# State-space stage of a two-block kernel: the next head's decay sums moved into the unit between two heads, the masked sums behind it, the output last

## What is computed

```python
xbc = silu(causal_depthwise_conv_2(xbc, conv_w, conv_b))
xs, b_in, c_in = jnp.split(xbc, [...], axis=-1)
a_cs = jnp.cumsum(a_dt, axis=-1)                      # one row per head
decay = jnp.exp(jnp.where(causal, a_cs[..., :, None] - a_cs[..., None, :], -jnp.inf))
cb = jnp.einsum('bclgn,bcsgn->bcgls', c_c, b_c)
y_diag = jnp.einsum('bcgjls,bcsgjp->bclgjp', cb[:, :, :, None] * decay, xdt)
decay_from_start = jnp.exp(a_cs).transpose(0, 1, 4, 2, 3)
y_off = jnp.einsum('bclgn,bcgjpn->bclgjp', c_c, prev) * decay_from_start[..., None]
y = (y_diag + y_off) + xs * d_skip
g = y * silu(z)
g = g * rsqrt(mean(g * g, axis=-1) + EPS) * norm_g    # per group of 256 channels
out = g @ w_out
```

## Time and profile before

| | |
|---|---|
| timed runs, median (lowest, highest) | 2892.21 us (2890.09, 2893.98) |
| the profiled execution, its own time | 2889.11 us |
| its span, first to last instruction | 2887.3 us |
| granted TensorE clock, mean | 0.944 of full |
| PE busy | 2724.0 us (94%) |
| DVE, ACT, POOL busy | 1184.7, 979.8, 925.4 us |
| state-space groups | about 1150 to 1612 us of the span |
| PE idle ahead of line 609 | 27.8 us, 15 times |

### The profile page before, as it was taken

The page is one execution under the profiler, slowest core; times in us unless marked ns, Lnnn a source line. Parts: engine busy times, 40 slices in busy tenths (PEclk is TensorE's granted clock), DMA queues, the critical chain, the costliest instruction groups (busy, mean ns, idle before and its releaser), DMA issues.

```text
span 2887.3 us, 35961 instructions
## 1 busy us (share of the span) xinstructions
PE 2724.0 (94%) x15144; PEld 2314.9 (80%) x15144; DVE 1184.7 (41%) x1641; ACT 979.8 (34%) x1482; POOL 925.4 (32%) x381
## 2 busy tenths in 40 slices
PE   4999999889999987989999999999979999999999
PEld 3777778667777767989988999999957677778887
DVE  5444442254444326676666431122343444422111
ACT  3333333333333333334434332233333433433222
POOL 2334344143343432222222334444320000244443
PEclk9999999999999998999999999999975766999999
DMA  3333233133332321111211223333210000133332
GB/s 114 90 92 104 85 111 88 51 100 96 96 100 91 97 78 51 53 52 59 59 52 52 76 82 93 92 92 89 77 51 8 15 8 15 54 93 95 95 95 88
DMA packets 61280, 215.65 MB, mean 75 GB/s; under 512 B 8128, under 2 KB 8512, under 8 KB 61120
## 3 DMA queue, kind: packets, MB, share of 16 engines
q1 hardware_dynamic: 55440, 199.78, 23.5%
q10 hardware_dynamic: 5680, 13.58, 1.4%
HBM read 211.24 MB, written 2.10 MB: 74 GB/s over the span
## 4 chain that ended last, share of the span: by engine, by line
PE 89%; DVE 6%; ACT 2%; issue 1%; ACTq 0%; POOL 0%; DMA 0%; DVEq 0%
PE psum L344 73%; PE psum L939 1%; PE psum L905 1%; PE psum L877 1%; PE psum L436 1%; PE psum L446 1%; PE psum L881 1%; PE psum L629 1%; PE psum L903 1%; PE psum L941 1%; PE psum L356 1%; PE psum L632 1%; PE psum L922 1%; PE psum L584 1%; DVE sb_scale L1483 1%
## 5 line engine op out<-in xcount | busy, mean ns | idle before, releaser
L324 POOL TENSOR_TENSOR sb_w_lo<-sb_w_raw,sb_w_hi 128x1024 fp32r<-128x1024 f32 x377 | 925.2, 2457 | 1939.9 <-ACT sb_w_hi L1055 1939.6
L344 PE MATMUL psum<-sb_h_hi,sb_w_hi 128*128 128x512 f32 (+1 forms) x2648 | 828.9, 355 | 74.6 <-DVE sb_h_lo L1492 45.9
L344 PE MATMUL psum<-sb_h_lo,sb_w_hi 128*128 128x512 f32 (+1 forms) x2648 | 801.1, 344 | 0.0
L344 PE MATMUL psum<-sb_h_hi,sb_w_lo 128*128 128x512 f32 (+1 forms) x2648 | 798.1, 343 | 0.0
L1055 ACT ACTIVATE sb_w_hi<-sb_w_raw 128x1024 fp32r<-128x1024 f32 x377 | 395.3, 1054 | 608.0 <-PE psum L344 458.7
L344 PEld LDWEIGHTS psum<-sb_h_hi,sb_w_hi 128*128 128x128 f32 x2648 | 466.5, 193 | 145.9 <-issue 60.6
L344 PEld LDWEIGHTS psum<-sb_h_lo,sb_w_hi 128*128 128x128 f32 x2648 | 464.3, 193 | 63.4 <-issue 7.5
L344 PEld LDWEIGHTS psum<-sb_h_hi,sb_w_lo 128*128 128x128 f32 x2648 | 463.8, 193 | 57.2
L344 PE MATMUL psum<-sb_mix_hi,sb_w_hi 128*128 128x264 f32 (+1 forms) x1424 | 416.9, 338 | 11.5 <-DVE sb_mix_lo L2193 5.8
L344 PE MATMUL psum<-sb_mix_lo,sb_w_hi 128*128 128x264 f32 (+1 forms) x1424 | 414.9, 337 | 0.0
L344 PE MATMUL psum<-sb_mix_hi,sb_w_lo 128*128 128x264 f32 (+1 forms) x1424 | 414.0, 337 | 0.0
(11 more groups left out here) (268 smaller groups left out, 2680.6 us busy)
## 6 DMA issues: line engine op xcount, KB each, us to landing
sb_w_raw<-in_weights SPq DMA_DIRECT2D x377, 512.0 KB, 3.6
sb_decay<-in_decay ACTq DMA_DIRECT2D x16, 640.0 KB, 3.9
sb_resid<-in_x ACTq DMA_DIRECT2D x1, 2048.0 KB, 11.7
out<-sb_resid SPq DMA_DIRECT2D x8, 256.0 KB, 2.0
sb_table<-in_rope_table ACTq DMA_DIRECT2D x1, 264.0 KB, 3.5
sb_s<-in_positions ACTq DMA_DIRECT2D x1, 256.0 KB, 5.7
sb_cols<-in_cols ACTq DMA_DIRECT2D x1, 158.5 KB, 7.1
sb_resid<-in_meta ACTq DMA_DIRECT2D x1, 64.0 KB, 11.8
```

Source lines behind the costliest of these rows:

```text
L324: e.tensor_tensor(g.w_lo[:, u % 4, :], g.w_raw[:, u % 2, :], g.w_hi[:, u % 4, :].bitcast(F32), ALU.subtract).then_inc(S["w_lo"], 1)
L344: mm = e.matmul(g.psum[0:m, at + b, 0:wd], w[:, slot, P * i:P * i + m], xs[:, tile, c:c + wd], start=first and n == 0, stop=last and n == 2)
```

## The change

In `pe_ssd` alone, in the loop over heads. The unit of eight blocks (48 matmuls) is cut into two halves of four blocks. The sums of decays of the next head stand between the halves; they stood behind the whole unit. The masked sums of the next head stand right behind the unit (at head 0 behind the total); they stood behind the output. The output of the head stands last. In the last group the pieces of the output projection are cut likewise. Nothing else moves, on no engine.

```diff
         for h in range(HG):
             if not last:
-                pe_ssd_unit(g, e, grp + 1, h)
+                pe_ssd_unit(g, e, grp + 1, h, range(4))
             elif h < 2:
-                pe_ssd_out(g, e, h, 0).then_inc(S["unit"], 1)
+                pe_ssd_out(g, e, h, 0, range(4))
             else:
-                pe_ssd_out(g, e, h - 2, 1, range(6))
+                pe_ssd_out(g, e, h - 2, 1, range(3))
+            if h < HG - 1:
+                pe_ssd_a(g, e, grp, h + 1)
+            if not last:
+                pe_ssd_unit(g, e, grp + 1, h, range(4, 8))
+            elif h < 2:
+                pe_ssd_out(g, e, h, 0, range(4, 8)).then_inc(S["unit"], 1)
+            else:
+                pe_ssd_out(g, e, h - 2, 1, range(3, 6))
             if h == 0 and grp:
                 e.wait_ge(S["state"], STEPS_OF_STATE * (grp + 1))
                 pe_ssd_total(g, e, grp - 1, 2)
             if h < HG - 1:
-                pe_ssd_a(g, e, grp, h + 1)
+                pe_ssd_mask(g, e, grp, h + 1)
             pe_ssd_y(g, e, grp, h)
-            if h < HG - 1:
-                pe_ssd_mask(g, e, grp, h + 1)
```

## The result

The kernel after the change took 2911.62 us, median of seven runs (2910.05 to 2921.15). The kernel before took 2893.6 beside it, median of seven (2890.09 to 2905.59). The ratio is 1.007 with a 95% interval of 1.0056 to 1.0085: slower by 18.0 us, where +17.8 and 2909 were forecast. The profiled execution of after took 2911.01 us and its span is 2909.2; before it was 2889.11 and 2887.3.

What follows compares the result with a forecast made beforehand. PE, busy 94% of the span, was taken to bound the kernel. Cover 12.4, seams 2.8 and clock 2.6 summed to +17.8 us; with 2891.3, the mean of all four times, that gave 2909 us, range 2898 to 2917.

Steps and rivals of the forecast that it cites:

- What bounds the place: Head 2, groups 1 to 6: the masked sums start 5.47 us after unit 1 ends, whatever PE does in between.
- Cover, +12.4: Head 2, groups 1 to 6: sums and output, 2.07 us of work, leave the wait, six times: +12.4 us.
- Clock, +2.6: Behind head 2's wait, groups 1 to 6: the lower clock costs 2.2 us each, 13.1 against 10.5 now: +2.6 us.
- The bound of 1.53 a time: Behind head 2's wait, groups 1 to 6: the clock's price can hardly fall below 1.53 us each.
- the rival with the dearer clock: Clock low for as long as in group 5 or longer at all six places: +4 to +8, 2913 to 2917; 12%.
- The rival in which the output does not stretch: Behind head 2's wait the output does not stretch at the lower clock, so the clock is cheaper: 2900; 8%.
- Seams, +2.8: Units behind an output take 0.20 us more, masked sums behind a unit 0.12 less where nothing waits: +2.8 us together.
- Last group: Head 2 of the last group: 7.9 us of PE work beside the chain either way, wait stays 1.7: 0.
- The other stages: Outside the state-space groups, which take some 18 us more, the other stages take nothing more.
- Other heads, POOL and DVE, at 0: Exponentials of heads 1 and 3 stay hidden; POOL meeting DVE's multiplies delays no user: 0, with 1.9 us of slack.
- The meeting at head 3: POOL's low part meets DVE's multiplies for head 3, which end some 6.8 us after unit 2; costed at 0.
- the rival of DVE coming late: Heads 3 or 1: POOL holds convolution steps too, 15 x 0.5 = 8 us, 2917; 4%.

Runs made afterwards that it cites:

- e1: The change with its second half undone: sums stay mid-unit, output ahead of the masked sums again at all heads; 2897.89 us, ratio 1.0022 to the kernel before.
- e2: The change everywhere but at head 1 of groups 1 to 7, where the output goes ahead of the masked sums again; 2899.41 us, ratio 1.0016.
- e8: The kernel before with masked sums ahead of the output at head 1 of groups 1 to 7 alone; 2913.49 us, ratio 1.0126.
- e7: The kernel before with the first half of unit 2 ahead of head 2's masked sums in groups 1 to 6; 2900.88 us, ratio 1.0072.
- e3: The kernel before with the norm's steps (Newton steps, normed tiles) ahead of the lift in DVE's program at head 1; 2875.72 us, ratio 0.9952.
- e5: e3 with ACT's two rsqrt steps moved between head 1's two exponentials; 2870.99 us, ratio 0.9969.
- e9: e5 with ACT's split moved ahead of head 1's exponentials in groups 1 to 7; 2866.73 us, ratio 0.9927.
- e4: The changed kernel with the norm's steps ahead of the lift in DVE's program at head 1; 2894.65 us, ratio 1.0021 to the kernel before.
- e6: e4 with ACT's two rsqrt steps moved between head 1's two exponentials; 2896.4 us, ratio 1.0034.
- e10: e6 with ACT's split moved ahead of head 1's exponentials in groups 1 to 7; 2876.98 us, ratio 0.996.

## Why the prediction was right

**What bounds the place: right.** The start of head 2's masked sums hangs on the end of unit 1 by 5.47 us, whatever PE does in between. Six arrangements of PE at an unchanged chain give 5.47 less the cover: 3.41 before (cover 2.07), 3.65 in e1 and e2 (output alone), 5.24 in e8 (sums alone), 5.48 after (none), 0.3 in e7 (cover 5.2). e3, e5 and e9 changed the chain instead and the wait went down to 1.65, 1.1 and nothing; in e4, e6 and e10 the same steps with the order of the change left 3.1, 3.1 and 1.75.

**Cover, +12.4: as forecast,** 6 x (5.48 - 3.41) = 12.4.

**Clock, +2.6: the mis-sized term, +1.4.** "I take the middle, 2.2 each" stood against 1.53 now. Masked sums and output took 1297.14 to 1301.61, 4.47 us; at full clock behind a wait they would take 0.65 + 1.83 = 2.48. So the price is 1.99 each, 11.9 for all six, against 10.5 before. The bound of 1.53 a time held, and no place had the price of group 5, 2.85. But every place had its length: the condition of the rival with the dearer clock, "low for as long as in group 5 or longer at all six", came true (6.8 us). Its price did not, because the fall came within the wait and 2.5 of the 6.8 us were idle, which the prediction had not thought of. The 2.2 was a middle between two values, and that it lies near 1.99 is luck. (What runs first behind the wait are the masked sums and then the output, not the output as the prediction says.) The rival in which the output does not stretch fell with the rows of 0.29.

**Seams, +2.8: near, +2.6 in groups 1 to 6 alone.** Forecast for these were 6 x (0.20 + 2 x 0.08) = 2.2. A unit behind an output takes 6.09, and masked sums behind a unit 0.46 instead of 0.58. The 2.6 is what is left of 16.45 when cover and clock are taken off, so errors of those two are in it. Group 0, three such seams, came out at +0.28 against 0.24.

**Last group, "the wait stays 1.7: 0": wrong by about 1.5.** The chain is as long as before, 9.6 us from the end of head 1's masked sums. The piece of the projection beside it now stands behind an output and takes the 0.2 of a seam more, so that the wait fell to 1.45. But the clock fell in the output behind it, which it had not done before behind 1.68. The chain there (start, us, what):

```profile
1601.55 0.15 PE psum L629 x2
...
1602.10 0.29 PE psum L632 x2
...
1603.57 3.15 PE psum L344 x18
```

The last group took 1.8 us more, against 0.36 of seams.

**Sum.** 16.45 + 0.28 + 1.8 = 18.5 in the stage against 17.8: -1.2 for the clock, +0.5 for the seams, +1.4 for the last group. That the misses nearly cancel is luck; the term that carries the forecast, the 12.4, was right on its own. The other stages were to give nothing; in the profiled pair they gave 3.3, and that is inside what they wander.

**Other heads, POOL and DVE, at 0: right in the sum, wrong in the piece that meets POOL.** Neither a multiply nor any other step of DVE for an output became a releaser of PE, and e2 has room for no more than the seams at the other heads. The meeting at head 3 came, but it held the last step of the convolution and not the multiply (DVE in the kernel after; alone that step takes 0.77):

```profile
1310.95 2.88 DVE L1822 SCALAR_TENSOR_TENSOR sb_xs<-sb_lift,sb_cols,sb_xs 128x528 f32<-128x528 f32 x1
...
1314.28 0.69 DVE L1879 TENSOR_TENSOR sb_part<-sb_part,sb_cbd 88x528 f32<-88x528 f32 x1
```

Head 3's multiplies ended at 1314.97, 7.1 us after unit 2 (1307.90), where 6.8 was forecast, and their user came at 1316.28: 1.3 us of slack instead of 1.9. So a convolution step held by POOL, the condition of the rival of DVE coming late, did occur in the change; DVE coming late did not. The head-1 meeting lies on the path once the chain is shortened (e4), and in e7 DVE was late at head 2, once the slack there was spent.

## What to carry to other kernels

Before a piece of work is moved on the engine that bounds, ask what it covers: work that stands between a producer's last result and a wait on a chain of other engines is cover, and where PE already waits there, taking it away costs its whole length, each time. Where it doesn't wait, as at the 17 other places here, it costs next to nothing. The other half is that the wait is mended at the chain and not with more cover: look at which instructions stand in the programs between the two ends only because of the order in which they are written, and move those (e3, e5, e9: -11.7, -18.9, -27.9 us in the stage). Read at each step what is late next, since it was an engine with 41% busy time that took the wait over.

## What the runs showed of the chip

- **POOL holds some steps of DVE and not others.** A DVE instruction with two tensors from SBUF that starts while POOL's 128x1024 low part runs ends only when that is through: in e5 POOL ran to 1281.05 and the Newton step to 1281.62, 2.78 us; in e6 the first step took 2.83, in e4 a multiply 2.81, in e7 one 2.77, each ending 0.5 to 0.6 us after POOL. In e9 a tensor_scalar with a single tensor from SBUF was held as well, 1.43 in place of 0.55, and ended 0.3 after POOL (1276.63). Steps that read PSUM were not held: in e9 the mean (`sb_mean<-psum`) started at 1274.86 beside the same low part and took its usual 0.71, and in the kernel after the skip step, with `sb_xs` and PSUM, took 0.77 beside POOL at 1301.65. The Trainium skill, "GPSIMD Engine Reference" (its table of figures, SBUF interfaces), names instructions with two SBUF inputs or in a 2-port mode of DVE. The four rows ahead agree; which mode the tensor_scalar was in, no run here shows.
- **Neither the length of a wait nor what stands behind it tells whether the clock falls.** In e3 the masked sums of head 2 wait 1.65 to 1.68 us in seven groups, with the same work behind them in groups 1 to 6. The granted clock fell behind four of the seven, in groups 1, 3, 5 and 7, and not in groups 2, 4 and 6. Windows of 6 us from the masked sums of groups 2 and 3:

```profile
1287.40:1293.40 6.00, 5.99 (x49) 5.99 (x50) 5.89 (x7) 2.40 (x7) 2.66 (x1) 1.00 0.01 3
1343.60:1349.60 6.00, 6.00 (x37) 6.00 (x38) 5.89 (x7) 2.39 (x7) 2.66 (x1) 0.72 0.00 0
```

  In the kernel before, the last group has the same order and the same 1.68 as in e3, and the clock stayed at 1.00. Of e10's six waits of 1.74 or 1.75, with an output behind each, it fell in four and not in two. It fell behind the 1.45 of the last group after the change, and at none of the seven waits of 1.1 in e5. What decides is left open.
- **The scatter has a place.** The ten executions of e1 lie in two bunches, 2887.83 to 2892.27 and 2903.51 to 2907.88, and its profile is one of the upper. Windows over the attention stage, the kernel before and then e1, show where its extra time lies:

```profile
2150.00:2600.00 450.00, 423.42 (x1811) 325.53 (x1810) 192.44 (x290) 159.78 (x320) 65.70 (x27) 0.78 0.11 31
```

```profile
2150.00:2600.00 450.00, 424.08 (x1748) 324.52 (x1749) 191.95 (x288) 159.05 (x319) 60.15 (x26) 0.73 0.10 30
```

  In the same 450 us PE was granted 0.78 in the one and 0.73 in the other, and got through 1811 records of matmuls against 1748. Ahead of that (0 to 1150) both have 0.97. The profile of e4, the other of the twelve with a rest as long (2455.2 us), shows 0.73 there too. The change does not touch this stage, so with a change of a few us one reads the stage that it touches, and not the span.
